# A hybrid mixer and mixture-of-experts step: bias rows laid into the outputs first, accumulating stores, own buffers for the last blocks, projections in equal thirds

## The reference, cut to what matters

```
h = layer_norm(x) * (1 + sc1) + sh1                       # x: 1024 sample tokens, 128 prompt tokens, 1024 wide
proj = h @ w_in                                           # the combined input projection
y = concat(gated linear attention, gMLP, short convolution, Fourier) @ w_out
x = layer_norm(ALPHA * x + g1 * y, ln1_g, ln1_b)
h = layer_norm(x) * (1 + sc2) + sh2
m = sum over the 8 chosen of 64 experts of  w_e * (silu(h @ gate_e) * (h @ up_e)) @ down_e   +  one shared expert
out = layer_norm(ALPHA * x + g2 * m, ln2_g, ln2_b)        # out = (v - mean) * rstd * ln2_g + ln2_b
```

## Time and profile before

| | us |
|---|---|
| median of three runs (lowest, highest) | 1798.75 (1797.79, 1806.94) |
| the profiled execution: its own time | 1792.3 |
| its span, first to last instruction | 1790.7 |
| PE busy / DVE busy / ACT busy / POOL busy | 1687.4 / 936.6 / 847.4 / 778.4 |

### The profile page before, as it was taken

How to read it: one execution, slowest core, us unless ns; L and a number is a source line. 1 busy time by engine, 2 the same in 40 slices (tenths; PEclk the granted TensorE clock), 3 DMA queues, 4 the chain that set the end, 5 groups by cost and what they waited for, 6 DMA issues and landing times.

```text
span 1790.7 us, 32687 instructions
## 1 busy us (share of the span) xinstructions
PE 1687.4 (94%) x8612; PEld 1317.1 (74%) x8613; DVE 936.6 (52%) x1466; ACT 847.4 (47%) x950; POOL 778.4 (43%) x445
## 2 busy tenths in 40 slices
PE   6999999999899899999999999999999999999944
PEld 2677778888455588888888787888888877878821
DVE  7532311158478885445546455454644655555528
ACT  2321012262032443556667667575656666767622
POOL 2230000300003555547556656676557566766620
PEclk9999999999999899999999999999999999999968
DMA  8515531020652374677979898898888888988776
GB/s 350 179 50 176 177 118 39 24 98 24 235 188 95 98 233 154 235 207 250 328 237 306 274 304 273 271 311 271 285 252 260 284 272 282 294 295 275 224 245 260
DMA packets 102448, 390.78 MB, mean 218 GB/s; under 512 B 21667, under 2 KB 38304, under 8 KB 74624
## 3 DMA queue, kind: packets, MB, share of 16 engines
q1 hardware_dynamic: 62576, 289.25, 43.7%
q0 software_dynamic: 37232, 91.44, 20.2%
q10 hardware_dynamic: 2592, 9.44, 1.9%
HBM read 339.94 MB, written 84.72 MB: 237 GB/s over the span
## 4 chain that ended last, share of the span: by engine, by line
PE 71%; DVE 9%; DMA 9%; issue 4%; ACT 3%; POOL 2%; ACTq 1%; SPq 1%; DVEq 0%; POOLq 0%
PE ps L884 38%; PE ps L2069 12%; DMA arena<-hx_dram,arena 6%; PE ps L939 5%; PE ps L2210 4%; PE ps L1992 2%; DMA acc_dram<-arena 2%; POOL d_split L619 1%; PE ps L916 1%; PE ps L2200 1%; PE ps L2042 1%; PE ps L2104 1%; DVE arena L1334 1%; PE ps L2165 1%; DVE small L1643 1%
## 5 line engine op out<-in xcount | busy, mean ns | idle before, releaser
L884 PE MATMUL ps<-gu_split,xT 128*128 (+1 forms) x2712 | 636.1, 390 | 0.1
L884 PEld LDWEIGHTS ps<-gu_split,xT 128*128 128x128 f32 x2712 | 508.5, 188 | 108.2 <-issue 3.0
L619 POOL TENSOR_TENSOR d_split<-raw,d_split (+1 forms) x65 | 299.4, 4607 | 153.2 <-ACT d_split L686 152.8
L884 PE MATMUL ps<-d_split,hTe 128*128 (+1 forms) x1356 | 341.3, 401 | 14.6 <-ACT arena L762 12.4
L1027 DVE TENSOR_TENSOR gu_split<-raw,gu_split (+1 forms) x130 | 293.3, 2298 | 97.8 <-ACT gu_split L681 97.8
L884 PEld LDWEIGHTS ps<-d_split,hTe 128*128 128x128 f32 x1356 | 249.3, 190 | 65.7 <-issue 18.9
L681 ACT ACTIVATE gu_split<-raw (+1 forms) x130 | 241.9, 1909 | 27.3 <-SPq L517 18.3
L650 POOL DMA_INDIRECT acc_dram<-arena x104 | 177.2, 1704 | 130.0 <-DVE arena L1204 100.0
L632 POOL DMA_INDIRECT arena<-hx_dram,arena x108 | 148.3, 1373 | 132.8 <-DVE arena L1199 102.6
L1193 DVE TENSOR_TENSOR arena<-ps,arena 128x256 f32<-128x256 f32 x113 | 70.4, 623 | 257.4 <-ACT arena L768 257.0
L1183 DVE TENSOR_TENSOR xT<-ps,xT 128x1024 fp32r<-128x1024 f32 x115 | 140.7, 1224 | 99.9 <-ACT xT L740 99.8
(11 more groups left out here) (317 smaller groups left out, 1435.9 us busy)
## 6 DMA issues: line engine op xcount, KB each, us to landing
raw<-w_exp_gate SPq DMA_DIRECT2D x64, 1024.0 KB
raw<-w_exp_up SPq DMA_DIRECT2D x64, 1024.0 KB
raw<-w_exp_down SPq DMA_DIRECT2D x64, 1024.0 KB, 7.0
arena<-w_ada SPq DMA_DIRECT2D x16, 1024.0 KB, 4.9
arena<-x_dram SPq DMA_DIRECT2D x18, 512.0 KB, 10.9
arena<-acc_dram SPq DMA_DIRECT2D x18, 512.0 KB, 11.3
arena<-ada_halves SPq DMA_DIRECT2D x4, 2048.0 KB, 24.4
w_raw<-w_in SPq DMA_DIRECT2D x16, 512.0 KB, 4.7
```

The costliest lines, as they stand in the source:

```text
L619: tt(d_split(q, 1), raw_d(q), d_split(q, 0).bitcast(F32), ALU.subtract).then_inc(d_low, 1)
L884: last = mm(dst, lhs(a, j), rhs(b, j), start=(t == 0), stop=(t == len(terms) - 1))
```

## The change

Four things change.

1. The projections go over `THIRDS = [(0, 3), (3, 6), (6, 9)]`: three groups of 384 columns, all in the split form; the plain float32 products for the prompt are gone. Where a third holds sample and prompt tiles, evacuations into the padded buffer `z` are made in two pieces.
2. The last two expert blocks: the second's `down` goes to banks 0 and 1 and waits for `xT_ready` instead of `y_ready`; ACT writes both results into `xg`, the gather buffer, which needs the last gathers landed (`xg_in`), and their scatter indices have their own columns, so neither ACT nor DVE waits for `y_out` there. POOL's scatter still does.
3. Near the start of phase 3 (right behind the load of `w_out`) SP stores `ln2_b`, broadcast, over all nine tiles of the outputs. In the last stage DVE's L1334 is gone; ACT scales the tile by the reciprocal in place (L850 after), and POOL adds it to the output with an indirect accumulating transfer (L681 after), where SP made a plain store. `ln2_b` is no longer loaded to SBUF.
4. A constant `fill` is added to the list rows of blocks past the end, so that their gathers find the empty list.

The diff, cut:

```diff
-        NG = len(GROUPS)
+        NG = len(THIRDS)
...
+            for i in range(NT):
+                dst = out_sample[0, tile(i), :] if i < ST else out_prompt[0]
+                sp.dma_start(dst, A["ln2_b"][0].partition_broadcast(P)).then_inc(bias_out, 16)
             sp.wait_ge(qk_ready, NT)
...
-            for i in range(NT):
-                sp.wait_ge(fin_ready, i + 1)
-                dst = out_sample[0, tile(i), :] if i < ST else out_prompt[0]
-                sp.dma_start(dst, acc_t[:, i, :]).then_inc(fin_out, 16)
...
+            pool.wait_ge(bias_out, 16 * NT)
+            for i in range(NT):
+                pool.wait_ge(fin_ready, i + 1)
+                dst, at = (out_sample[0], i) if i < ST else (out_prompt[0], 0)
+                pool.indirect_dma_start(out=dst, out_offset=bass.IndirectOffsetOnAxis(ap=row_i[:, at:at + 1], axis=0),
+                                        in_=acc1_t[:, i, :], in_offset=None, compute_op=ALU.add).then_inc(fin_out, 16)
...
+            def last_out(b, p, j, u):
+
+                act.wait_ge(y_mm, b + 1)
+                act.wait_ge(xg_in[p], 8 * last + 48)
+                a(xg[:, p, :].rearrange("p (h x) -> p h x", h=2), ps[:, LAST_BANK[u]:LAST_BANK[u] + 2, :], ACT.Copy,
+                  scale=w_t[:, bass.ds(j, 1)]).then_inc(y_ready, 1)
...
-            for i in range(NT):
-                ln_std(2 * NT + i, acc_t[:, i, :])
+            for i in range(NT + 1):
+                if i < NT:
+                    ln_std(2 * NT + i, acc_t[:, i, :])
+                if i:
+                    r = (i - 1) % 2
+                    act.wait_ge(scale_ready, i)
+                    a(acc1_t[:, i - 1, :], acc1_t[:, i - 1, :], ACT.Copy, scale=lrec[:, r:r + 1]).then_inc(fin_ready, 1)
...
-                at_least(pe, y_ready, b)
+                if bank == 4:
+                    at_least(pe, y_ready, b)
+                else:
+                    pe.wait_ge(xT_ready, b + 3)
...
-                    scale = ln_scale(2 * NT + i)
-                    stt(acc_t[:, i, :], acc1_t[:, i, :], scale, ln2_row[:, 1, :], ALU.mult, ALU.add).then_inc(fin_ready, 1)
+                    r = i % 2
+                    dve.wait_ge(std_ready, 2 * NT + i + 1)
+                    if i >= 2:
+                        dve.wait_ge(fin_ready, i - 1)
+                    dve.reciprocal(lrec[:, r:r + 1], lstd[:, r:r + 1]).then_inc(scale_ready, 1)
...
-                    elif g < 2:
-                        terms = [(part(a, j), hT[:, b, j, cols]) for j in range(KD) for a, b in TERMS]
                     else:
-                        terms = [(raw[:, j, :], hT_prompt[:, j, :]) for j in range(KD)]
+                        terms = [(part(a, j), hT[:, b, j, cols]) for j in range(KD) for a, b in TERMS]
```

More of the change, by code:

```diff
@@ L43 @@
 _at = 0
-for _n, _w in (("ident", P), ("cum", 2 * P), ("suf", 2 * P), ("mask", 4 * P), ("tri", P), ("key", E + 1), ("order", E),
+for _n, _w in (("ident", P), ("cum", 2 * P), ("suf", 2 * P), ("mask", 4 * P), ("tri", P), ("key", E + 1), ("order", E), ("fill", 1),
                ("low8", NGRP * NGRP), ("blk", NBP), ("tokid", NT), ("base", E), ("emptylist", 2 * P)):
@@ L77, in constants @@
     put("key", np.concatenate([np.tile(key(f), (E, 1)), key(e)], 1).astype(np.float32))
+    put("fill", np.where(e == E - 1, float(E * T // P), 0.0).astype(np.float32))
     put("order", np.tile(np.array(rank_at())[None, :], (P, 1)).astype(np.float32))
@@ L407, in build @@
         tok_b = table(NT, BF16).rearrange("p (i c) -> p i c", c=2)
+        row_i = table(NT, I32)
         h_sb = table(2 * FF).rearrange("p (r f) -> p r f", r=2)
@@ L577, in phase3_sync @@
             sp.wait_ge(d_low, NE - 1)
-            for k, n in enumerate(("ln2_g", "ln2_b")):
-                sp.dma_start(ln2_row[:, k, :], A[n][0].partition_broadcast(P)).then_inc(row_ready, 16)
+            sp.dma_start(ln2_row[:, 0, :], A["ln2_g"][0].partition_broadcast(P)).then_inc(row_ready, 16)
             sp.dma_start(g2_row[0], mod_dram[0, 3 * D:4 * D].partition_broadcast(P)).then_inc(row_ready, 16)
@@ L642, in phase3_pool, with scatter @@
                                         in_offset=bass.IndirectOffsetOnAxis(ap=list_row[0:n, c:c + 1], axis=0)).then_inc(list_in, 16)
-            def scatter(b, p, j):
+            def scatter(b, p, j, rows=yb, ix=0):
                 pool.wait_ge(y_ready, b + 1)
@@ L667, in phase3_pool @@
             for u in range(2):
-                scatter(NT + last + u, (NT + u) % 2, last + u)
+                scatter(NT + last + u, (NT + u) % 2, last + u, rows=xg, ix=2)
             for p in range(2):
@@ L926, in down @@
                 for h in range(2):
-                    last = products(ps[:, 4 + h, :], lambda s, c: hTe[:, p, s, c * P:(c + 1) * P],
+                    last = products(ps[:, bank + h, :], lambda s, c: hTe[:, p, s, c * P:(c + 1) * P],
                                     lambda s, c: v[s][:, c, h * 512:(h + 1) * 512], 2)
@@ L1005, in phase3_pe @@
             for u in range(2):
-                down(NT + last + u, (NT + u) % 2, last + u)
+                down(NT + last + u, (NT + u) % 2, last + u, LAST_BANK[u])
             for i in range(1, NT):
@@ L1310, in phase3_dve @@
             for u in range(2):
[L1311 to L1313 removed]
+                next_scatter((NT + u) % 2, last + u, ix=2)
+            dve.wait_ge(row_ready, 16 * (8 + 2))
             for s in range(NT + 1):
@@ L1572, in _ @@
                     act.wait_ge(conv_done, 2)
-                for g, (i0, i1) in enumerate(GROUPS):
+                for g, (i0, i1) in enumerate(THIRDS):
                     r = NG * n + g
@@ L1578, in _ @@
                     if name == "cvc":
-                        off = 1 if i0 < ST else 3
-                        a(z[:, c, i0 * P + off:i1 * P + off], src, ACT.Copy).then_inc(evac_a, 1)
+                        for t0, t1, off in parts_of(i0, i1):
+                            last = a(z[:, c, t0 * P + off:t1 * P + off], src[:, (t0 - i0) * P:(t1 - i0) * P], ACT.Copy)
+                        last.then_inc(evac_a, 1)
                     elif name == "lr":
@@ L1792, in _ @@
                         dve.wait_ge(ring_mm, r + 1)
-                        dve.tensor_tensor(dst, ps[:, 2 + r % 4, 0:(i1 - i0) * P], dst, ALU.mult).then_inc(evac_d, 1)
+                        for dst, t0, t1 in pieces:
+                            last = dve.tensor_tensor(dst, ps[:, 2 + r % 4, (t0 - i0) * P:(t1 - i0) * P], dst, ALU.mult)
+                        last.then_inc(evac_d, 1)
                 if name == "cvx":
```

37 lines of the change are left out of this document (19 added, 18 removed).

## The result

The changed kernel took 1807.58 us (median of 20 runs, 1802.39 to 1814.97) against 1800.05 us for the kernel before (20 runs, 1794.66 to 1812.94). The ratio is 1.0036, 95% interval 1.0023 to 1.0049: 6.5 us slower, which is a real difference and lies within the 0.5% that the prediction calls no change. The profiled execution took 1802.83 us, with a span of 1801.0.

A forecast was written before the change was run, and what follows sets the result against it. PE bounds most of the chain (71%), with DVE and the DMA queues both nearly full in the last stage. Projections -0.7, drain -4.9 and last stage +5.9 sum to +0.3 us: 1799.0 us forecast, range 1786 to 1812.

The forecast's parts named there:

- Projections, spacing: Projections: 384-column matmuls follow one another in 171.3 ns, the larger of two bounds plus a remainder; -6.5 us.
- the line between the rows: Projections: 384-column spacing on a straight line between the 128- and 512-column rows, 189.5 ns; +15.4 us.
- the skill's shape: Projections: a line between the Trainium skill's gaps, 81 and 131 ns, gives 114 ns; the change would cost some 10 us.
- Modulation tiles: Projections: PE waits for each chunk's second modulation tile, 0.8 us in seven chunks, about 0.2 in the first; +5.8 us.
- The stage: Projections as a whole, spacing and waits for modulation tiles together: -0.7 us.
- Bias rows: Early stores of the bias behind `w_out`: 11.5 us of transfer, but nothing waits for them; 0.
- Drain: Last two expert blocks: the last scatter is issued earlier, so the last stage's loads start earlier; -4.9 us.
- Last stage: Last stage: DVE quicker per tile, but accumulating stores at 2.65 us a tile delay tile 8's loads; +5.9 us.
- cheap stores: Last stage: accumulating stores cost as little as plain ones beside loads; -3.6 there, total -9.2 us, 1789.5; chance 0.14.
- Dear ones: Last stage: accumulating stores cost nearer 4 us each; +14.0 there, total +8.4 us, 1807; chance 0.1.
- The spacing rival: Projections: 384-column spacing follows the line, 189 ns; total +19.2 us, 1818; chance 0.13.
- U and E: Stretches from the projections' end to the first block scatter, and on to the loop's last but one: no change, 0.

The follow-up runs named there:

- again: The changed kernel, unchanged, run and profiled a second time: ratio 1.0024 to the kernel before.
- Number 6: Against the kernel before: the drain's own buffers, old last stage, and thirds with one modulation tile after every second third instead of two per chunk; ratio 0.9941.
- numbers 1 and 2: First: changed kernel with the old last stage, no early bias rows, 0.9960 to before. Second: kernel before with the drain's own buffers and banks alone, 0.9962.
- number 4: Changed kernel with its nine final stores by POOL not accumulating, so outputs lack the bias row; ratio 0.9958 to the kernel before.
- number 10: Kernel before with drain buffers, thirds with spread modulation tiles, and the changed last stage for tiles 1 to 5 only; ratio 0.9924.
- number 9: Kernel before with drain buffers, thirds with spread modulation tiles, and the changed last stage for tiles 2 to 5 only; ratio 0.9900.
- number 8: Kernel before with drain buffers, thirds with spread modulation tiles, and the changed last stage for tiles 3 to 6 only; ratio 0.9922.
- number 3: Changed kernel with POOL starting no final store before the loads of all nine tiles have landed; ratio 1.0003 to the kernel before.
- number 5: Changed kernel with non-accumulating final stores, the last two of the nine issued by SP instead of POOL; ratio 0.9924 to the kernel before.
- number 7: Drain buffers, thirds with spread modulation tiles; last stage: ACT scales tiles 0 to 6, POOL adds bias in SBUF, SP stores plainly; ratio 0.9968 to before.

## Why the prediction came out as it did

The verdict, no change of 0.5%, was right, and so was the main mechanism: a quicker DVE and drain, paid for by stores that take the DMA engines from the loads. But luck had a part in the verdict: in the first pair of traces the touched stages sum to 8.8 us more than forecast, against the 9 us that count as no change. The measured time, 1807.6, lies in the range, 8.6 us above the 1799.0 predicted. The steps:

- **Projections, spacing:** 171.3 ns forecast, 173.3 measured; at 1.2 us for each ns this is -4.1 instead of -6.5. The rule "the larger of two bounds plus a small remainder" was nearly right; the line between the rows (189.5) and the skill's shape were not.
- **Modulation tiles:** +5.8 forecast, the wait seen at the place and in the size named. With the stage at +0.8 and the spacing at -4.1 the waits come to 4.9 (the view of waits has 4.3). Number 6 shows it: without them P falls by 4.8. The forecast took 5.1 us to landing where the earlier trace rows has a median of 4.9, which gives 4.8 by the same sum; its lower bound of 3.5 comes to 3.9. The stage: -0.7 forecast, +0.8 (again +0.5).
- **Bias rows 0:** no wait for them shows, and U is no shorter in numbers 1 and 2, which lack them. The dip of the clock, 1.2 us, was not in the forecast; it comes without the rows too.
- **Drain:** -4.9 forecast, -5.4 and -6.1 in the traces; -4.2 with `ln2_b` still loaded. The step named the missing load as a reason for its bound of -7.
- **Last stage:** this is the step that failed in size, +5.9 forecast, +13.7 and +12.1 measured. The accumulating store, 2.65 us a tile from one row of both queues, was right (2.62), and tile 8's loads landed 49.6 us after the first issue where 50.4 was worked out. Three things were missed. PE's sum was priced at the 3.67 us of a busy PE, but behind an idle time of over 6 us the granted clock was 0.58 and it took 6.37 (+2.7; in the second execution 0.71 and 5.17, +1.5). The last store goes out 0.7 us later than worked out (7.5 us behind tile 8's start instead of 6.8), and lands 0.4 us slower. And "landing 6.5 us later" was taken for the end of the span, while 4.8 us follow where POOL issued the last transfer. 2.7 less the 0.8 of the loads, 1.1 and 4.8 make the 7.8 that were missing.

Of the rivals, cheap stores (1.28 us a tile) fell by row and by number 4, which shows what they would have been worth: 14 us. Dear ones, nearer 4 us, fell too, though their time of 1807 was hit, for other reasons. The spacing rival fell. U and E, put at 0, stray by some us in every kernel; but for the 1.2 us of the dip, no run gives a reason to charge that to the change.

Open: why TensorE's clock dips at 385 to 400 us in some variants and not in others; what passes in the 4.8 us behind POOL's last landing (whether SP sees the semaphore late, or POOL's program ends late), and whether a store of POOL's without a row index has them; and number 10 against number 9.

## What to carry to other kernels

A transfer that adds on its way cost twice a plain one here, in the time of all DMA engines: use it where they idle, not beside loads that the chain waits for, and mix the two ways tile by tile if one engine and the DMA are both nearly full. Let the last transfer of a program be one that SP issues, and let POOL's last indexed store land at least some 4 us before it (an estimate: 4.5 to 4.9 us behind the one less 0.4 to 0.8 behind the other; number 8 against number 9). When PE's work gets shorter, look at each load that was just in time before: here spreading those products, so that two thirds lie between them, gave back 4.8 us.

## What the runs showed of the hardware

- An accumulating store of 512 KB by row index cost all 16 DMA engines 2.62 us beside loads (changed kernel); alone they landed 2.66 us apart (number 3). The same store without accumulation cost 1.28 (number 4).
- The span ended 4.7 to 4.9 us behind the last landing where it was an indexed store of POOL's, 0.4 to 0.8 us where it was SP's; in number 8, where SP's came 2.5 us behind POOL's, 4.5 us behind POOL's.
- Eight f32 matmuls of 128x512 took 3.6 to 3.7 us at a granted clock of 1.00 with up to 1.76 us of idle time ahead of them, and 5.17 to 6.71 us behind 2.5 to 6.8 us (0.71 to 0.55). The time does not follow the length of the idle stretch: 6.71 us came behind 3.8 us (number 5), 5.17 behind 6.5. One of number 7, 2.20 us behind the last, had 0.68 and 5.37, while another there, 2.21 us behind, had 1.00: the idle time just ahead does not decide it alone.
- 384-column matmuls with a weight load each followed one another in 173.3 ns, 512-column ones in 224.6, 128-column ones, as the prediction works out from the earlier trace rows, in 119.
- A DVE operation with two SBUF inputs (number 7) took 3.06 instead of 1.28 us beside a POOL addition of 3.33.
